# Leaving 48 instead of 32 tokens out of the dense expert pass of a PEER layer (one core)

## The chip, the cores and the metric

One core of a Trainium2 chip runs the whole program in one launch. The metric is the time of one execution in microseconds (us), the median over several executions. TensorE is called PE here, VectorE DVE, ScalarE ACT, GpSimd POOL and the sync engine's queue SP.

## What is computed

A residual block for 512 tokens of width 1024, in float32. After two kinds of attention and a LayerNorm comes a PEER layer: for every token, 8 heads choose 16 of 16384 experts each, so 128 experts a token, and sum their outputs.

```python
q = (xt @ w_q).reshape(T, PEER_HEADS, 2, half)
s1 = jnp.einsum('thd,hnd->thn', q[:, :, 0], keys1)
s2 = jnp.einsum('thd,hnd->thn', q[:, :, 1], keys2)
v1, i1 = lax.top_k(s1, 16); v2, i2 = lax.top_k(s2, 16)
cand = v1[..., :, None] + v2[..., None, :]         # 256 a head
sc, pos = lax.top_k(cand.reshape(T, 8, 256), 16)   # 16 experts a head, eidx
gate = jax.nn.softmax(sc, axis=-1)
a = jnp.einsum('nhkd,nd->nhk', u_tab[eidx], x)
w = jax.nn.gelu(a, approximate=False) * gate
y = jnp.einsum('nhk,nhkd->nd', w, v_tab[eidx])
x = layer_norm(ALPHA * x + y)
```

## The kernel before

The attention half ends at about 240 us and the change does not touch it. Then the 512 tokens are treated in two ways.

**Gathered tokens.** For the first 128 tokens (block 0, one token on each partition) the chosen rows of both tables are fetched. For each of the 128 ranks POOL issues one indirect DMA (line L822) that brings 128 rows of 4 KB, 0.524 MB, into one of 8 slots of `rows`. For `u_tab` DVE multiplies such a slot with x and sums it (`dot`, L1454), for `v_tab` it adds it with its weight to y (`add_row`, L1860). Of the 128 u ranks, 16 ("extra") are left for the second half of the program, where they have buffers of their own (`extra_row`, L864; `extra_dot_of`, L1848).

**Dense tokens.** For the other 384 tokens PE multiplies the whole table. The u pass goes over 128 tiles of 128 experts. Each tile is split into a high and a low float32r part (ACT `split_hi` L495, POOL `split_lo` L501, 4 slots ahead of PE), and `features` (L1964 to L1966) does 8 x 3 matmuls for it, whose moving side is the tokens. ACT takes the gelu (L1106) and stores it to DRAM. The gates of a chunk of 32 tokens are scattered into a dense array with one-hot matmuls: DVE builds the one-hots for groups of 8 tokens (`one_hots`, L1688 and L1692), PE multiplies them (`scatter`, L2237 and L2238), ACT stages the result and SP stores 2 MB a chunk. The v pass goes over 128 tiles too: DVE multiplies gelu and gate (L1802), the product is split (L1199, L1811), and PE adds 18 matmuls of 512 columns a tile (L2019 to L2021) into PSUM.

**Late tokens.** The last 32 of the 384 dense tokens are left out of the u pass, so a matmul there has 352 columns. In their 32 columns the gelu scratch holds ones. Their activations are computed from gathered rows: four groups of 32 partitions hold the same 32 tokens and a quarter of their ranks each, so 32 gathers and 32 dots do all of them. For this the numbers, the gates and at the end the products gelu x gate are moved between partitions (`move_numbers`, `move_gates`, `move_weights`, L625 to L645, four small copies from SBUF to SBUF each). The products are scattered in place of the gates, in the last groups of the last chunk, as three bf16 parts (`late_hots` L1717 and L1721, `late_scatter` L2251) and not two fp16 parts as in the other groups.

**The order.** Each engine runs its own list, written out by hand, and waits on semaphores. The u pass is: 44 tiles (`A_PRE`) beside which DVE finds the experts (`search_list`, `route_block`), six rounds of 12 tiles (`two_chunks`) with 8 scatter groups and 16 gathers each, and 12 last tiles. `turn_chosen` (L2212) transposes numbers and gates on PE at the first tile of round 0. `FIRST_GROUPS_AFTER = (2, 3, 4, 5)` puts the first four scatters of round 0 behind tiles 46 to 49; `GROUP_AFTER = (0, 1, 3, 4)` does it in every other half round. POOL gathers by tables: `FIRST_ROWS_AT` (32 rows at tiles 13 to 43), `LATE_ROWS` (round 0) and `MID_ROWS` (2, 1, 1, repeated). When the dots pass from one set of tokens to another, ACT copies the other x into PSUM (`home`, L1139) in front of a round. In the v pass an octet is 8 tiles with 8 v gathers, one load of gates (1.5 MB), two of gelus (0.75 MB) and 8 of v tiles (0.5 MB). `v_octet` (L866) and `octet` (L1870) take the extra ranks: two in octets 0 and 1, one in octets 2 to 13.

Of the kernel before, what the change touches and what calls it, by code (L numbers as in the profile page):

```python
# [103 lines left out]
LATE_ROWS = (0, 0, 0, 2, 3, 3, 2, 2, 2, 2, 2, 2)  # L104
# [4 lines left out]
SHARE_GAPS = 8, 9, 10  # L109
LIST_SLOTS = 4  # L110
# [14 lines left out]
def build(nc, x_t, x_rows, w1, w_ff, b_f, sinks, ln_par, w_pq, keys_t, u_t, u_rows, v_tab, consts, out):  # L125
    g_dram = nc.dram_tensor("g_scratch", (CHUNKS, P, ETILES, CHUNK), F32, kind="Internal").ap()
    a_dram = nc.dram_tensor("gelu_scratch", (ETILES // 4, P, 4, DENSE), F32, kind="Internal").ap()
    c_dram = nc.dram_tensor("decay_scratch", (4, HEADS, SEQ), F32R, kind="Internal").ap()

    ctx = ExitStack()  # L130
    with ctx:
# [106 lines left out]
        late_parts = row_weight[:, LATE_TOKENS:].bitcast(BF16).rearrange("p (m t two) -> p m t two", m=3, two=2)  # L238
# [136 lines left out]
        extra_gathered = [sem(f"extra_gathered{i}") for i in range(2)]  # L375
# [11 lines left out]
        late_numbers_ready = sem("late_numbers_ready")  # L387
        late_numbers_moved = sem("late_numbers_moved")
# [164 lines left out]
        EXTRA_ASKED_AT, EXTRA_DOT_AT = (2, 4), (5, 7)  # L553

        def extra_rows(j, par, at):

            if isinstance(j, int) and j == 0:
                return {k: (2 * par + i, i) for i, k in enumerate(at)}
            return {at[1]: (2 * j + (2 + par), par)}
# [18 lines left out]
        def _(sp):  # L578
# [1795 lines left out]
```

## Time and profile before

| what | value |
|---|---|
| time of the runs, median (range) | 1434.01 us (1432.85 to 1437.87) |
| time of the profiled execution | 1433.48 us |
| its span, first to last instruction | 1431.8 us |
| PE, PE weight loads, DVE | 1406.7, 1248.2, 1087.3 us busy |
| ACT, POOL | 606.7, 903.4 us busy |
| DMA | 415.41 MB in 138959 packets |

The profile names instructions by engine and line of the source, with what they write and read. A matmul row has the partitions and columns of what moves through PE; its duration reaches from the first column to a modelled end, and the next matmul starts well before it. So the pace of PE is read from the starts of successive rows. The brackets behind a row give how long the engine sat idle before it and what released it.

### The profile page before, as it was taken

The numbers are of one execution on the slowest core, as the hardware profiler recorded it, in microseconds if no ns is written. First come the engines' busy times: TensorE is split into PE (matmuls) and PEld (weight loads), VectorE is DVE, ScalarE is ACT, GpSimd is POOL, SyncE is SP. The second block draws the span as 40 slices with busy tenths as digits, with TensorE's granted clock in tenths as the row PEclk, the third lists the DMA queues.
The fourth block names the chain that finished last, engine by engine and source line by source line (L and its number), as shares of the span: only waits on it lengthen the run. The fifth ranks groups of instructions, "written<-read, shape, count | busy, mean of one in ns | idle before, by whom it ended". The sixth has DMA issues, their size and how long they took to land.

```text
span 1431.8 us, 24761 instructions
## 1 busy us (share of the span) xinstructions
PE 1406.7 (98%) x8045; PEld 1248.2 (87%) x8045; DVE 1087.3 (76%) x2324; ACT 606.7 (42%) x1019; POOL 903.4 (63%) x595
## 2 busy tenths in 40 slices
PE   9999999999999999999999999999999999999996
PEld 5888878888999999999999999878888888888885
DVE  5366666688999998858774885987777777777786
ACT  5666751324333354454544443333333333333332
POOL 3422331335599978979888786766666666666744
PEclk9999999999999999999999999999999999999998
DMA  6213120423689979999999899999999999999981
GB/s 243 75 50 113 59 90 1 147 84 102 197 316 342 323 259 395 417 389 418 418 417 399 341 381 407 383 388 387 371 374 374 372 366 360 367 368 366 372 315 59
DMA packets 138959, 415.41 MB, mean 290 GB/s; under 512 B 13904, under 2 KB 56656, under 8 KB 136720
## 3 DMA queue, kind: packets, MB, share of 16 engines
q1 hardware_dynamic: 80128, 240.69, 45.9%
q0 software_dynamic: 42064, 151.15, 26.8%
q10 hardware_dynamic: 16704, 22.81, 4.3%
q8 instruction: 29, 0.48, 0.1%
q14 instruction: 34, 0.28, 0.1%
HBM read 363.89 MB, written 50.14 MB: 289 GB/s over the span
## 4 chain that ended last, share of the span: by engine, by line
PE 76%; DVE 8%; DMA 5%; POOL 4%; issue 3%; ACT 2%; SPq 1%; DVEq 0%; ACTq 0%; POOLq 0%
PE banks L2019 12%; PE banks L2021 11%; PE banks L2020 11%; PE banks L1964 11%; PE banks L1965 11%; PE banks L1966 11%; DMA raw<-v_tab 3%; POOL lo L501 2%; PE banks L2081 2%; PE banks L2237 1%; PE banks L2238 1%; POOL rows L822 1%; PE banks L2174 1%; DMA rows<-u_rows,expert_at 1%; DVE rows L1454 1%
## 5 line engine op out<-in xcount | busy, mean ns | idle before, releaser
L501 POOL TENSOR_TENSOR lo<-raw,hi 128x1024 fp32r<-128x1024 f32 x224 | 540.2, 2413 | 416.5 <-ACT hi L495 396.5
L1964 PE MATMUL banks<-x1T_hi,hi 128*128 128x352 f32 (+3 forms) x1168 | 389.9, 334 | 1.3 <-ACT kept L1106 1.0
L1965 PE MATMUL banks<-x1T_lo,hi 128*128 128x352 f32 (+3 forms) x1168 | 384.6, 329 | 0.0
L1966 PE MATMUL banks<-x1T_hi,lo 128*128 128x352 f32 (+3 forms) x1168 | 383.6, 328 | 0.0
L495 ACT ACTIVATE hi<-raw 128x1024 fp32r<-128x1024 f32 x291 | 305.6, 1050 | 57.0 <-DMA raw<-u_t 37.4
L2019 PE MATMUL banks<-hi,wgt_hi 128*128 128x512 f32 x750 | 292.1, 389 | 2.0 <-DVE wgt_lo L1811 1.9
L2020 PE MATMUL banks<-lo,wgt_hi 128*128 128x512 f32 x750 | 291.8, 389 | 0.0
L2021 PE MATMUL banks<-hi,wgt_lo 128*128 128x512 f32 x750 | 291.8, 389 | 0.0
L1964 PEld LDWEIGHTS banks<-x1T_hi,hi 128*128 128x128 f32 x1168 | 219.8, 188 | 6.2 <-ACT kept L1106 1.3
L1966 PEld LDWEIGHTS banks<-x1T_hi,lo 128*128 128x128 f32 x1168 | 220.3, 189 | 4.4
L1965 PEld LDWEIGHTS banks<-x1T_lo,hi 128*128 128x128 f32 x1168 | 220.1, 188 | 3.9
L1454 DVE CUSTOM_DVE_ANT_0 rows<-rows,banks 128x1024 f32<-128x1024 f32 x144 | 172.5, 1215 | 61.0 <-DMA rows<-u_rows,expert_at 47.8
L1199 ACT ACTIVATE wgt_hi<-wgt 128x384 fp32r<-128x384 f32 x125 | 65.6, 525 | 313.1 <-PE banks L2021 284.4
L2019 PEld LDWEIGHTS banks<-hi,wgt_hi 128*128 128x128 f32 x750 | 140.8, 188 | 32.2 <-DVE wgt_lo L1811 2.7
L2021 PEld LDWEIGHTS banks<-hi,wgt_lo 128*128 128x128 f32 x750 | 140.8, 188 | 29.4
L2020 PEld LDWEIGHTS banks<-lo,wgt_hi 128*128 128x128 f32 x750 | 140.8, 188 | 29.2
L1860 DVE SCALAR_TENSOR_TENSOR banks<-rows,row_weight,banks 128x1024 f32<-128x1024 f32 x128 | 164.1, 1282 | 0.7
L822 POOL DMA_INDIRECT rows<-v_tab,expert_at x128 | 142.2, 1111 | 29.4 <-issue 21.1
L1811 DVE TENSOR_TENSOR wgt_lo<-wgt,wgt_hi 128x384 fp32r<-128x384 f32 x125 | 76.9, 616 | 108.6 <-ACT wgt_hi L1199 93.0
L822 POOL DMA_INDIRECT rows<-u_rows,expert_at x144 | 140.5, 975 | 28.8 <-issue 23.0
L1106 ACT ACTIVATE gelu<-banks 128x352 f32<-128x352 f32 x116 | 53.8, 464 | 241.4 <-PE banks L1966 229.1
L501 DVE TENSOR_TENSOR lo<-raw,hi 128x1024 fp32r<-128x1024 f32 x67 | 83.9, 1252 | 4.5 <-ACT hi L495 4.4
(245 smaller groups left out, 1846.7 us busy)
## 6 DMA issues: line engine op xcount, KB each, us to landing
raw<-u_t SPq DMA_DIRECT2D x128, 512.0 KB
raw<-v_tab SPq DMA_DIRECT2D x128, 512.0 KB
g_scratch<-stage SPq DMA_DIRECT2D x12, 2048.0 KB
gelu_scratch<-gelu ACTq DMA_DIRECT2D x116, 192.0 KB
ga<-gelu_scratch SPq DMA_DIRECT2D x29, 768.0 KB
gg<-g_scratch SPq DMA_DIRECT2D x14, 1536.0 KB
raw<-w SPq DMA_DIRECT2D x26, 512.0 KB
raw<-w_pq SPq DMA_DIRECT2D x16, 512.0 KB
```

What stands on the lines that cost most here:

```text
L495: act.activation(parts_of(c)[0][:, :], raw[:, c % RAW_SLOTS, :], ACT.Copy).then_inc(hi_ready, 1)
L501: eng.tensor_tensor(l[:, :], raw[:, c % RAW_SLOTS, :], h[:, :].bitcast(F32), ALU.subtract).then_inc(odd_lo_ready if by_vector(c) else lo_r ...
L822: pool.indirect_dma_start(rows[:, k % ROWS, :], None, table, at).then_inc(gathered[k % ROWS], 16)
L1454: dve.tensor_tensor_reduce(rows[:, k, :], rows[:, k, :], x1_home, 1.0, 0.0, ALU.mult, ALU.add, dots8[:, k:k + 1]).then_inc(row_used, 1)
L1811: dve.tensor_tensor(l[:, :], wgt[k % 2][:, :], h[:, :].bitcast(F32), ALU.subtract).then_inc(wgt_lo_ready, 1)
L1860: dve.scalar_tensor_tensor(y0, rows[:, k, :], row_weight[:, bass.ds(ROWS * r + k, 1)], y0, ALU.mult, ALU.add).then_inc(row_used, 1)
L1964: pe.matmul(o, h[:, s], hiT[:, k, tokens], start=(k == 0), stop=False)
L1965: pe.matmul(o, h[:, s], loT[:, k, tokens], start=False, stop=False)
L1966: ins = pe.matmul(o, l[:, s], hiT[:, k, tokens], start=False, stop=(k == KT - 1))
L2019: pe.matmul(o, h_at(b), h[:, s], start=start, stop=False)
L2020: pe.matmul(o, h_at(b), l[:, s], start=False, stop=False)
L2021: ins = pe.matmul(o, l_at(b), h[:, s], start=False, stop=stop)
```

## The change

It has five parts.

1. **48 late tokens.** `LATE_TOKENS` goes from 32 to 48 as `LATE_SETS = (32, 16)`. Matmuls of the u pass have 336 columns, gelu activations too, and 48 columns of ones stand in the scratch. The second set of 16 tokens lies eight times on the partitions, so 16 more u gathers and dots belong to late tokens, 48 in all.
2. **16 extra ranks more for the v pass.** `EXTRA` goes from 16 to 32, so the u pass still has 144 gathers and dots. In the v pass an octet takes 2 extra ranks in octets 0 and 1, 3 in octets 2 to 5 and 2 in octets 6 to 13. A third buffer (`extra2`) lies over the gelu slots. The ranks are turned into weights in two batches of 16.
3. **Transfers through DRAM.** Numbers, gates and weights are stored to DRAM with one DMA for each set and loaded in the other layout with another. The x of the second set is stored eight times in front of the u pass and loaded in round 0 into `sel`.
4. **Order.** `turn_chosen` goes from tile 44 to tile 45, the first dots of round 0 go behind one more group of one-hots (`FIRST_DOTS`), and `LATE_ROWS` starts one tile later. There are homes for x before rounds 0, 2 and now 3, and the weights are stored in round 4 and not behind round 2.
5. **Two more late groups.** 6 instead of 4 of the last 8 scatter groups are late ones, and `late_part_free` lets a late group use one-hot buffers of the round before.

```diff
-LATE_TOKENS = 32
-SPREAD = P // LATE_TOKENS
+LATE_SETS = (32, 16)
+LATE_TOKENS = sum(LATE_SETS)
 LATE_AT = P - LATE_TOKENS
-LATE_RANKS = RANKS // SPREAD
+LATE_RANKS = sum(RANKS // (P // n) for n in LATE_SETS)
 FEATURED = DENSE - LATE_TOKENS
-EXTRA = 16
+EXTRA = 32
+EXTRA_BATCHES = (16, 16)
...
-LATE_ROWS = (0, 0, 0, 2, 3, 3, 2, 2, 2, 2, 2, 2)
+LATE_ROWS = (0, 0, 0, 0, 2, 3, 3, 3, 3, 2, 2, 2)
+FIRST_DOTS = (0, 2, 2, 2, 2, 3, 2, 3)
+CHOSEN_AT = 1
+FIRST_BATCH_AT = 8
...
             n = 3 * (group - WHOLE_GROUPS) + m
-            used_by = n // 2 if n < len(late_slots) else WHOLE_GROUPS + (n - len(late_slots)) // 3
+            if n < len(late_slots):
+                used_by = n // 2 - (HOT_SLOTS if n // 2 >= WHOLE_GROUPS else 0)
+            else:
+                used_by = WHOLE_GROUPS + (n - len(late_slots)) // 3
             return 2 * (used_by + 1)
...
-        EXTRA_ASKED_AT, EXTRA_DOT_AT = (2, 4), (5, 7)
+        ASKED_AT = {2: (2, 4), 3: (0, 2, 4)}
+        DOT_AT = {2: (4, 6), 3: (2, 4, 6)}
...
-            def move_numbers():
+            def store_numbers():
 
                 sp.wait_ge(late_numbers_ready, 1)
-                for g in range(SPREAD):
-                    sp.dma_start(late_numbers[late_group(g), :],
-                                 block_numbers[LATE_AT:, late_group(g)]).then_inc(late_numbers_moved, 16)
+                for i, n, tokens, columns in late_sets():
+                    sp.dma_start(turn_dram[0][i].rearrange("g t c -> t g c"),
+                                 block_numbers[tokens, :].rearrange("t (g c) -> t g c", c=n)
+                                 ).then_inc(late_numbers_stored, 16)
+
+            def load_numbers():
+
+                sp.wait_ge(late_numbers_stored, 16 * LATE_MOVES)
+                for i, n, tokens, columns in late_sets():
+                    sp.dma_start(late_numbers[:, columns], turn_dram[0][i].rearrange("g t c -> (g t) c")
+                                 ).then_inc(late_numbers_moved, 16)
...
-                        if first and tile == 0:
+                        if first and tile == CHOSEN_AT:
                             take_turned()
...
-            v_octet(0, 0)
-            v_octet(0, 1)
-            with pool.Fori(1, OCTETS // 2 - 1) as i:
-                v_octet(i, 0)
-                v_octet(i, 1)
+            v_octet(0, 0, 2)
+            v_octet(0, 1, 2)
+
+            for slot in range(GELU_SLOTS):
+                pool.wait_ge(gelu_stored[slot], 16 * (A_PRE + A_MID) // GELU_SLOTS)
+            with pool.Fori(1, 3) as i:
+                v_octet(i, 0, 3)
+                v_octet(i, 1, 3)
+            with pool.Fori(3, OCTETS // 2 - 1) as i:
+                v_octet(i, 0, 2)
+                v_octet(i, 1, 2)
...
-                    if first and tile == 0:
+                    if first and tile == CHOSEN_AT:
                         turn_chosen(at)
```

**First place: the start of round 0 on DVE.** `is_i` are the one-hots of the numbers, `gate_hi` and `gate_lo` those times the gates; the first row copies the gates to PSUM. Before:

```order
L1669 COPY banks<-gate_lo 128x384 [waits gate_step]
L1688 TENSOR_TENSOR is_i_0<-banks,selT 128x1024 [waits gate_step]
L1692 TENSOR_TENSOR gate_hi<-is_i_0,banks 128x1024 [waits is_i1_ready]
L1692 TENSOR_TENSOR gate_lo<-is_i_0,banks 128x1024
L1688 TENSOR_TENSOR is_i_0<-banks,selT 128x1024 [waits onehot_ready]
L1688 TENSOR_TENSOR is_i_1<-banks,selT 128x1024
L1454 ISA rows,small<-rows,banks 128x1024 [waits dots8_free,gathered0,homes_ready]
```

And with the change, from the same copy on:

```order
L1766 COPY banks<-gate_lo 128x384 [waits gate_step]
L1785 TENSOR_TENSOR is_i_0<-banks,selT 128x1024 [waits gate_step]
L1789 TENSOR_TENSOR gate_hi<-is_i_0,banks 128x1024 [waits is_i1_ready]
L1789 TENSOR_TENSOR gate_lo<-is_i_0,banks 128x1024
L1785 TENSOR_TENSOR is_i_0<-banks,selT 128x1024 [waits onehot_ready,homes_ready]
L1785 TENSOR_TENSOR is_i_2<-banks,selT 128x1024
L1551 ISA rows,small<-rows,banks 128x1024 [waits dots8_free,gathered0]
```

The third group's one-hots now stand in front of the first dot. Nothing in front of the first group moved (some repeated rows between are not shown).

**Second place: the last round on DVE,** from the second group of one-hots on. Before, it is followed by dots and by two more groups of this kind:

```order
L1747 CAST row_weight<-small 128x64 [waits late_step]
L1688 TENSOR_TENSOR is_i_0<-banks,selT 128x1024 [waits onehot_ready,scattered,late_step]
L1688 TENSOR_TENSOR is_i_1<-banks,selT 128x1024
L1692 TENSOR_TENSOR gate_hi<-is_i_0,banks 128x1024 [waits is_i1_ready]
L1692 TENSOR_TENSOR gate_lo<-is_i_0,banks 128x1024
```

With the change the group behind its dots is already a late one:

```order
L1814 TENSOR_TENSOR is_i_0<-banks,selT 128x1024 [waits onehot_ready,scattered]
L1814 TENSOR_TENSOR is_i_2<-banks,selT 128x1024
L1818 TENSOR_TENSOR gate_hi<-is_i_0,sel 128x1024 [waits scattered,is_i1_ready]
L1818 TENSOR_TENSOR gate_lo<-is_i_0,sel 128x1024 [waits scattered]
L1818 TENSOR_TENSOR gate_hi<-is_i_0,sel 128x1024 [waits scattered]
```

Groups 2 and 3 have three products instead of two, each with a wait for PE, and the parts they read lie in `sel`.

## Rows read from the trace of the kernel before

**Rows 1.** Windows: length, busy PE, PEld, DVE, ACT, POOL, clock, DMA share, GB/s.
```profile
600.00:760.00 160.00, 160.00 (x1240) 156.88 (x1239) 121.29 (x206) 76.87 (x123) 136.45 (x92) 1.00 1.01 411
893.00:970.00 77.00, 75.03 (x330) 61.23 (x329) 69.41 (x76) 26.72 (x36) 53.25 (x40) 1.00 1.02 387
1099.60:1132.20 32.60, 32.60 (x146) 26.99 (x145) 24.61 (x31) 11.82 (x16) 20.73 (x16) 1.00 0.98 372
1130.00:1140.00 10.00, 10.00 (x46) 8.29 (x45) 7.42 (x10) 3.59 (x5) 7.62 (x5) 1.00 1.03 421
```

**Rows 2.** Timeline of PE: start, duration; first and last of 36, 21 and 45 matmuls.
```profile
599.74 0.32 PE L1964 MATMUL banks<-x1T_hi,hi 128*128 128x352 f32 x1
605.34 0.32 PE L1966 MATMUL banks<-x1T_hi,lo 128*128 128x352 f32 x1
...
329.95 0.39 PE L1964 MATMUL banks<-x1T_hi,hi 128*128 128x512 f32 x1
334.48 0.39 PE L1966 MATMUL banks<-x1T_hi,lo 128*128 128x512 f32 x1
...
252.21 0.27 PE L1964 MATMUL banks<-x1T_hi,hi 128*128 128x128 f32 x1
257.12 0.27 PE L1966 MATMUL banks<-x1T_hi,lo 128*128 128x128 f32 x1
```

**Rows 3.** Timeline of DVE from the last routing steps to the first one-hots.
```profile
516.63 0.68 DVE L1639 TENSOR_TENSOR sel<-sel,gsum 128x512 f32<-128x512 f32 x1
517.23 2.48 DVE L1612 SCALAR_TENSOR_TENSOR dots_gelu<-sel 128x128 f32<-128x128 f32 x1
524.65 2.30 DVE L1664 CAST gate_hi<-selT 128x768 f16<-128x768 f32 x1
530.85 0.68 DVE L1692 TENSOR_TENSOR gate_lo<-is_i,banks 128x1024 f16<-128x1024 f16 x1
```

**Rows 4.** What DVE waited for from 350 to 530 us: total, times, longest.
```profile
DVE best L1487 <- ACT scores L1074: 0.6, 1, 0.6
DVE work L1584 <- DVE cand L1579: 0.5, 1, 0.5
```

**Rows 5.** Timeline of PE: the first scatter.
```profile
532.39 0.23 PE L2237 MATMUL banks<-gate_hi,is_i 128*128 128x128 f16 x1
```

**Rows 6.** Timeline of POOL: splits, gathers and its wait for the numbers.
```profile
455.37 2.41 POOL L501 TENSOR_TENSOR lo<-raw,hi 128x1024 fp32r<-128x1024 f32 x1
457.94 0.96 POOL L822 DMA_INDIRECT rows<-u_rows,expert_at  x1 [0.16 <-issue]
458.92 4.77 POOL L501 TENSOR_TENSOR lo<-raw,hi 128x1024 fp32r<-128x1024 f32 x2
523.86 0.19 POOL L815 COPY expert_at<-small 128x8 uint32<-128x8 uint32 x1 [4.29 <-DMA small<-row_weight]
```

**Rows 7.** Timeline of the last round: ACT, DVE, then PE.
```profile
791.70 0.18 ACT L1192 ACTIVATE small<-banks 128x32 f32<-128x32 f32 x1
793.07 1.29 DVE L1688 TENSOR_TENSOR is_i<-banks,selT 128x1024 f16<-128x1024 f16 x2
794.87 0.68 DVE L1692 TENSOR_TENSOR gate_lo<-is_i,banks 128x1024 f16<-128x1024 f16 x1
809.81 3.29 DVE L1721 TENSOR_TENSOR gate_hi<-is_i,row_weight 128x1024 bf16<-128x1024 bf16 x1
833.35 3.29 DVE L1721 TENSOR_TENSOR gate_lo<-is_i,row_weight 128x1024 bf16<-128x1024 bf16 x1
840.84 0.23 PE L2251 MATMUL banks<-gate_lo,is_i 128*128 128x128 bf16 x1
842.13 0.22 PE L2251 MATMUL banks<-gate_lo,is_i 128*128 128x128 bf16 x1
```

**Rows 8.** Waits of ACT: the first from 866 to 900 us, the second from 900 to 1000.
```profile
ACT hi L495 <- DMA raw<-u_t: 11.9, 4, 6.7
...
ACT hi L495 <- DMA raw<-v_tab: 9.5, 4, 4.4
```

More of the change, by code:

```diff
@@ L551, in shared_norm, with extra_number_of, early_extras, late_sets @@
             return SHARED.index(n)
-        EXTRA_ASKED_AT, EXTRA_DOT_AT = (2, 4), (5, 7)
[L555 to L559, printed above, removed]
+        ASKED_AT = {2: (2, 4), 3: (0, 2, 4)}
+        DOT_AT = {2: (4, 6), 3: (2, 4, 6)}
+        def extra_number_of(i, each, q):
+            return (2 * i + (EXTRA_BATCHES[0] - 12 + q) if each == 2 else 3 * i + (q - 2)) if not early_extras(i) else 2 * i + q
+        def early_extras(i):
+            return isinstance(i, int) and i < 2
+        def late_sets():
+            first, column = P, 0
+            for i, n in enumerate(LATE_SETS):
+                first -= n
+                yield i, n, slice(first, first + n), slice(column, column + n)
+                column += n
         def lagging(step, lag, j, first):
@@ L647, in two_chunks @@
+            def two_chunks(o, first=False, weights=False):
                 for t in range(MID_TILES):
@@ L1161, in late_dots_done, with two_chunks @@
                 act.activation(late_gelu, late_dots, ACT.Gelu).then_inc(late_gelu_ready, 1)
-            def two_chunks(o, first=False, second=False, last=False):
+            def two_chunks(o, first=False, second=False, third=False, last=False):
                 for half in range(2):
@@ L1176, in two_chunks @@
                         if second and tile == 0:
+                            second_home()
+                        if third and tile == 0:
                             late_dots_done()
@@ L1750, in _, with two_chunks @@
             one_hots(0, 0, True)
-            def two_chunks(o, first=False, second=False, last=False):
+            def two_chunks(o, homes=None, first=False, last=False):
                 for tile in range(8):
@@ L1758, in two_chunks @@
                         one_hots(tile + 1, o, first and tile + 1 < HOT_SLOTS)
-                    if first and tile == 0:
-                        dve.wait_ge(homes_ready, 3)
-                    if second and tile == 0:
-                        dve.wait_ge(homes_ready, 4)
-                    for n in (2 * tile, 2 * tile + 1):
+                    if homes is not None and tile == 0:
+                        dve.wait_ge(homes_ready, homes)
+                    done = sum(FIRST_DOTS[:tile]) if first else 2 * tile
+                    for n in range(done, done + (FIRST_DOTS[tile] if first else 2)):
                         dot(n % ROWS, 2 * o + (R_PRE + n // ROWS))
@@ L2257, in two_chunks @@
                     at = tile % 4, 3 * o + (A_PRE // 4 + tile // 4)
-                    if first and tile == 0:
+                    if first and tile == CHOSEN_AT:
                         turn_chosen(at)
```

192 lines of the change are left out of this document (129 added, 63 removed).

## The prediction

> **What bounds the kernel now.** I read the busy times first, then windows and pace, then who waits for whom. PE is busy nearly all the time, and between 600 and 760 us all of it [rows 1], so the time is PE's list plus its few stalls. A busy PE tells nothing of its pace; that is read from starts [rows 2]. In the u pass 36 matmuls of 352 columns start within 5.60 us, one each 160.0 ns. With 512 columns it is 4.53 us for 20 steps, 226.5 ns. The slope is 66.5 ns for 160 columns, 0.416 ns a column. The next limits stand close behind. In front of round 0 it is DVE: from 350 to 530 us it waited 0.6 us at most for anything [rows 4], so the end of routing and the first one-hots come when DVE has done its list, whatever PE does. POOL is second: a split and a gather take 2.41 and 0.96 us with small gaps, 3.55 us a tile (455.37 to 458.92) [rows 6], against 24 x 0.160 = 3.84 us of PE. Third are the DMA engines, with shares of 0.98 to 1.03 from round 1 to the end [rows 1].
>
> **Part 1, the columns (-20.4 us).** A matmul loses 16 columns, 16 x 0.416 = 6.65 ns, a tile 0.16 us, so it takes 3.68 us; 128 tiles x 24 = 3072 matmuls give 20.4 us. This holds if the pace follows the columns down to 336. What could forbid it is the weight load, which every matmul keeps whatever its columns. PE's weight loads are busy 156.88 of 160 us in the u pass [rows 1]. But matmuls of 128 columns, with loads of the same size, start each 111.6 ns [rows 2], far under the 153 ns wanted here, so the loads overlap. The Trainium skill, page Perfetto Trace Analysis, section Identifying the Most-Contended Engine, judges TensorE by the busy share of its weight loads. By it PE is at 98% of a limit that the change doesn't touch, and part 1 would be nothing; that is rival C.
>
> **Front of round 0 (+5.6 us).** PE's first scatter stands behind tile 46 before and after and needs the first one-hots. DVE ended them at 530.85 + 0.68 = 531.5 us [rows 3], PE started at 532.4 [rows 5]. With the change PE would come 47 x 0.16 = 7.5 us earlier, but in DVE's list nothing in front of these one-hots has moved, only behind them. So PE waits until 531.5 at the latest: 0.9 us of the 7.5 stay, 6.6 are lost. Two rows of DVE are much longer than their size asks for: 2.48 us for 128 elements, 2.30 us for a cast [rows 3], both while POOL splits. POOL's next split now waits longer for the late numbers, and one of the two may come free, about 1 us. I take a loss of 5.6, bounds 4 and 7.5. Moving the transposes to tile 45 costs nothing: that wait was under 1 us, and PE now waits at the scatter. POOL's stalls at tiles 13 to 21 (a tile with two gathers costs it about 4.8 us against 3.68) are covered by the same wait.
>
> **Late numbers and gathers (+1.0 us).** POOL waited 4.29 us for the numbers, until 523.86 [rows 6]. Now two stores, a wait and two loads stand in that place, and SP has them in front of its next tile loads. No row shows a load behind a store here; the nearest is that POOL wait, the whole of a copy with its four issues, so I put the numbers 0 to 4.3 us later, at about 526. In front of tile 55 POOL then has 2, 3, 3, 3, 3, 2, 2 gathers, 18 x 1.25 us, and 8 splits x 2.41: it ends the split of tile 55 at about 568, and PE wants it at about 568. Queued behind it is only the next split. I take 1 us, bounds 0 and 3. The gates, the second x, its home before round 3 and the weights have a round of slack each: nothing, since DVE is busy 121.29 of 160 us [rows 1].
>
> **Two more late groups (+0.9 us on PE).** 24 matmuls instead of 16 a group: 1.29 us for 23 steps, 56 ns each [rows 7], 16 x 56 = 0.9 us.
>
> **The same on DVE (+3.5 us).** In the last round DVE may start only when ACT has taken the weights (791.70). A normal group takes 793.07 to 795.5, 2.4 us; the late ones take 5.9, 6.4, 4.3 and 5.8, mean 5.6, because some products last 3.29 instead of 0.68 us [rows 7]. DVE ended the last at 833.35 + 3.29 = 836.6, PE wanted it at 840.84, 4.2 us later [rows 7]. Two groups turned late add 2 x 3.2 = 6.4 us to DVE, and the first one's third product waits for scatter 1, 0.5 us. PE comes 11 x 0.16 = 1.8 us earlier and is 0.9 longer. Stall: 6.9 - 4.2 + 1.8 - 0.9 = 3.6, say 3.5. Bounds: 0, if the products fall beside POOL's work more luckily (0.68 each), and 6.
>
> **From the last round to octet 1 (+2.5 us).** ACT waited for tiles 11.9 and 9.5 us here [rows 8], PE stood 1.97 of 77 us between 893 and 970, at a DMA share of 1.02 [rows 1]. The bytes stay the same, so the 12 last u tiles can't come in 1.9 us less, and DVE starts its last 16 dots later. I take 2.5, bounds 0 and 5.
>
> **The extra ranks (+4 us).** 16 more gathers of 0.524 MB; at the 421 GB/s of a full window [rows 1] each takes 1.25 us of all engines. An octet takes 32.6 us and moves 372 GB/s at a share of 0.98 [rows 1]; full windows read 1.02 to 1.03, so 4 to 5%, 1.3 to 1.7 us, are free. One more rank (octets 6 to 13) just fits. Two more (octets 2 to 5) are 2.5 us, over by 0.8 to 1.2, times 4 octets, with no slack carried from before since PE stood before 970. I take 4, bounds 0 and 20 (16 x 1.25, nothing free). DVE and POOL have room: 24.61 and 20.73 of 32.6 us [rows 1], plus at most 2 x 2.5 us each.
>
> **Sum.** 1433.5 of the profiled execution - 20.4 + 5.6 + 1.0 + 0.9 + 3.5 + 2.5 + 4.0 = 1431.1 - 0.5 for stalls counted twice (a PE that waits in one place lets the DMA engines catch up for the next) = 1430.6 us. That execution is 0.5 us under the median of the runs, which I leave alone.
>
> **Rivals.** *A: the queues absorb it.* The stalls of the last round, of the way to octet 1 and of the v pass stay near nothing, since tiles are split 4 ahead and loads have several us of slack; then 1433.5 - 20.4 + 5.6 + 1.0 + 0.9 = 1420.6, about 1422. For it: PE is busy through the whole octet shown, at 372 GB/s where another window moves 421 [rows 1]. Against: the shares near 1. The same section of the Trainium skill's page calls the occupancy of the 16 DMA engines misleading and goes by bandwidth; by it 12% are free and every extra rank fits, which is this rival. Chance 0.20.
>
> *B: the v pass becomes DMA-bound, slower.* The place is octets 2 to 13, the price 1.25 us for each of 16 ranks. It decides from the point at which the share of 0.98 means that nothing is free: then all octets stretch, and instead of 4 us it is 16 to 20. 1430.6 + 12 = 1442.6. For it: the window at 1.02 already had PE standing. Against: another reads 1.03 with 421 GB/s [rows 1]. Chance 0.20.
>
> *C: PE is bound by weight loads.* Part 1 is 0, and so are the losses that come from an earlier PE: 1433.5 + 0.9 + 2 + 4 = 1440.4. Against it the 111.6 ns. Chance 0.03.
>
> *D: gathers fall behind in rounds 0 and 1,* since POOL has 0.1 us of slack a tile instead of 0.3: up to 5 us more, 1435.6. Chance 0.07.
>
> **Chances.** What a measurement of this kernel can tell from no change is about 0.3%, 4.3 us: faster is under 1429.7, slower over 1438.3. My forecast has 0.50, and since its terms scatter by some us and its value lies near that line, 0.17 of it is faster and 0.33 the same. A gives 0.20 faster, B 0.18 slower and 0.02 the same, C 0.03 slower, D 0.05 the same and 0.02 slower. Sum: faster 0.37, same 0.40, slower 0.23. The range reaches to A and to B, 1421 to 1443; the forecast's own is 1426 to 1436.
>
> **What would show it.** Starts of 336-column matmuls each 153 ns. PE idle by 4 to 7 us just before its first scatter, with DVE's one-hots as releaser. POOL's wait for the numbers ending near 526. In the last round PE waits for late one-hots of groups 5 to 7. From 970 to about 1090 us PE shows small stalls and DMA shares over 1.0, with 400 GB/s. I am wrong if the pace stays at 160 ns, if the first scatter comes well before 530 us, or if the v pass takes 1.5% more or not a bit more than before.

## The result and the profile after

| | median us | runs | ratio to before, 95% interval |
|---|---|---|---|
| before | 1434.4 | 1432.85 to 1437.87 | |
| the change | 1461.8 | 1458.45 to 1468.88 | 1.0199, 1.0166 to 1.0233 |

The change makes the kernel 2.0% slower, where 1430.6 us was forecast. The profiled execution of the changed kernel spans 1467.2 us (time 1468.88) against 1431.8, 35.4 us more. It is the longest of the four runs; by the medians the loss is 27.4. From here on all stretches are of profiled executions, and the table places the 35.4 us: u tiles by the start of their gelu on ACT, octets by the start of their first cast of the weights on ACT.

| point | before | after | lag | lost on the way | predicted loss |
|---|---|---|---|---|---|
| u tile 0 | 353.3 | 352.8 | -0.5 | | |
| u tile 49 | 547.0 | 544.6 | -2.4 | 5.9 | 5.6 |
| u tile 56 | 578.8 | 581.1 | +2.3 | 5.8 | 1.0 |
| u tile 102 | 785.6 | 781.5 | -4.1 | 1.0 | 0 |
| u tile 105 | 799.3 | 801.1 | +1.8 | 6.4 | 0 |
| u tile 116 | 850.1 | 851.1 | +1.0 | 1.0 | 4.4 |
| u tile 127 | 893.7 | 898.1 | +4.4 | 5.2 | 2.5 |
| end | 1431.8 | 1467.2 | +35.4 | 31.0 | 4 |

"Lost" is the change of the lag plus the 0.16 us that each tile should gain. The gain itself is there. In the timeline of PE in the changed kernel (start, duration) these are the first and last of 17 matmuls, 2.46 / 16 = 153.8 ns each against 160.0 in [rows 2]. Undisturbed gelus of the last 12 tiles follow each other in 3.68 us instead of 3.84, so 127 tiles bring 20.3 us.

```profile
564.74 0.31 PE L2075 MATMUL banks<-x1T_lo,hi 128*128 128x336 f32 x1
...
567.20 0.32 PE L2076 MATMUL banks<-x1T_hi,lo 128*128 128x336 f32 x1
```

All of it and 35 us more is lost. Of the 31.0 us behind the last u tile, 3.0 are lost before octet 2, 26.1 in octets 2 to 14, and 2.0 in the end of the program, which no run isolates. The octets:

| octet | 0 | 1 | 2 | 3 to 5 | 6 to 12 | 13 | 14 |
|---|---|---|---|---|---|---|---|
| before | 32.9 | 33.8 | 33.8 | 32.64 | 32.64 | 32.7 | 32.6 |
| after | 36.4 | 32.6 | 35.0 | 34.0 to 34.2 | 35.0 to 35.2 | 34.5 | 34.1 |
| extra ranks after (before) | 2 | 2 | 3 (1) | 3 (1) | 2 (1) | 2 (1) | 0 |

Octets 3 to 5 with three extra ranks lose less than octets 6 to 12 with two. The bytes of the ranks alone can't do that. The window of one octet of the changed kernel, to be read against the third line of [rows 1] (busy PE, PEld, DVE, ACT, POOL, then clock, DMA share, GB/s):

```profile
1171.50:1206.70 35.20, 33.29 (x146) 26.91 (x146) 28.89 (x36) 11.86 (x17) 23.56 (x17) 1.00 0.94 359
```

PE stands 1.9 of 35.2 us, and the DMA engines move less than before, 359 GB/s at 0.94 instead of 372 at 0.98. Neither DVE (28.9) nor POOL (23.6) is full. So this is a chain of waits. The waits of that octet (total, times, longest), and of PE from 1000 to 1415 us:

```profile
POOL lo L524 <- ACT hi L518: 9.1, 3, 4.4
ACT wgt_hi L1286 <- DVE wgt L1899: 8.2, 2, 4.7
DVE extra L1945 <- DMA extra<-u_rows,small: 2.3, 1, 2.3
PE banks L2129 <- DVE wgt_lo L1908: 1.9, 2, 1.5
...
PE banks L2129 <- DVE wgt_lo L1908: 18.9, 19, 1.5
```

The timeline of the octet, first POOL's, then DVE's:

```profile
1178.53 1.80 POOL L936 DMA_INDIRECT extra<-u_rows,small  x1 [0.30 <-issue]
1186.63 1.86 POOL L936 DMA_INDIRECT extra<-u_rows,small  x1 [0.30 <-issue]
1189.41 2.40 POOL L524 TENSOR_TENSOR lo<-raw,hi 128x1024 fp32r<-128x1024 f32 x1 [0.92 <-ACT hi L518]
1199.39 2.40 POOL L524 TENSOR_TENSOR lo<-raw,hi 128x1024 fp32r<-128x1024 f32 x1 [4.43 <-ACT hi L518]
...
1190.03 2.86 DVE L1945 CUSTOM_DVE_ANT_0 extra<-extra,x 128x1024 f32<-128x1024 f32 x1 [2.35 <-DMA extra<-u_rows,small]
1192.82 0.55 DVE L1908 TENSOR_TENSOR wgt_lo<-wgt,wgt_hi 128x384 fp32r<-128x384 f32 x1
1198.27 1.21 DVE L1945 CUSTOM_DVE_ANT_0 extra<-extra,x 128x1024 f32<-128x1024 f32 x1
1199.42 2.78 DVE L1908 TENSOR_TENSOR wgt_lo<-wgt,wgt_hi 128x384 fp32r<-128x384 f32 x1
```

POOL asks for the first extra row at 1178.53. Its dot stands two tiles later in DVE's order, behind tile 4, and DVE reaches it 9.2 us after the ask; the row lands 11.5 us after it, at 1190.03. DVE has stood 2.35 us with the weights of tile 4 queued behind. It then runs beside POOL's splits: the dot takes 2.86 us instead of 1.21, a `wgt_lo` 2.78 instead of 0.55. POOL's split had begun 0.03 us ahead of that one and lasted 2.40; DVE's instruction ended 0.4 us behind it. The Trainium skill, page SBUF — State Buffer, section SBUF: two separate sides, says that a shared port pair is an exclusive lock: a DVE operation with two SBUF inputs or a GpSimd operation that reads SBUF, whichever starts first, has it for the whole instruction, and the other fully blocks. These rows agree: `wgt_lo` reads `wgt` and `wgt_hi`, and it ended 0.4 us behind the split. PE waits 1.5 and 0.4 us in this octet, both times for a `wgt_lo`. The end of this chain, shares of the span, on the changed kernel's page:

```profile
PE 26%; DVE 23%; DMA 17%; issue 17%; POOL 12%; ACT 3%; DVEq 0%; POOLq 0%; SPq 0%; ACTq 0%
```

In the u pass the losses sit at tiles 55 and 103 and at the end. Windows of the changed kernel there (columns as above), and what PE waited for from 778 to 800 us:

```profile
576.00:584.00 8.00, 5.79 (x47) 5.32 (x45) 8.00 (x13) 3.66 (x7) 7.57 (x6) 0.99 1.03 417
584.00:588.00 4.00, 3.51 (x25) 3.51 (x26) 3.98 (x9) 1.26 (x3) 3.52 (x4) 0.59 1.04 418
784.00:788.00 4.00, 2.08 (x14) 1.80 (x12) 0.00 (x0) 0.12 (x1) 0.99 (x2) 1.00 1.04 419
788.00:792.00 4.00, 2.44 (x9) 2.47 (x10) 0.21 (x1) 3.40 (x6) 2.84 (x2) 0.59 1.02 415
792.00:796.00 4.00, 4.00 (x18) 4.00 (x17) 3.85 (x9) 0.00 (x0) 0.48 (x1) 0.56 1.04 416
796.00:800.00 4.00, 4.00 (x37) 3.88 (x36) 4.00 (x7) 2.37 (x4) 2.24 (x2) 1.00 0.28 103
...
PE banks L2388 <- ACT stage L1230: 3.5, 1, 3.5
```

PE stands 2.2 us from 576 to 584 and 3.5 from 784 to 792. Behind each stall the granted clock is 0.56 to 0.59 for 4 and 8 us, near the lower of its two levels (1.2 of 2.4 GHz), and that costs again: 18 matmuls start from 792 to 796, 37 from 796 to 800. PE waited for ACT, and ACT for tiles:

```profile
574.79 1.06 ACT L518 ACTIVATE hi<-raw 128x1024 fp32r<-128x1024 f32 x1 [6.79 <-issue]
787.88 1.06 ACT L518 ACTIVATE hi<-raw 128x1024 fp32r<-128x1024 f32 x1 [5.97 <-DMA raw<-u_t]
```

(The first wait has the label issue, so the trace doesn't show what ended it. ACT's next ones, until 589 us, are for tiles, and the DMA engines are full, with a share of 1.03 from 576 on.) One round of the u pass, tiles 90 to 102, in DMA numbers, before and after:

```profile
DMA packets 6201, 21.80 MB, mean 404 GB/s; under 512 B 689, under 2 KB 2224, under 8 KB 5944
DMA packets 6710, 21.75 MB, mean 418 GB/s; under 512 B 1267, under 2 KB 2722, under 8 KB 6455
```

Before, a round moved 21.8 MB in 53.9 us. Now it moves as much in 52.0 at 418 GB/s; no window of 52 us that was read went over 419. And 52.0 us is also PE's own list of a round (8 tiles of 4.66 us, 4 of 3.68). Such windows between 604 and 797 us read 399 to 419 GB/s (before 395 to 419, with 1.9 us more for each round), so little slack is left from round 0 on, and none where it is 418.

### The profile page after: what moved, and what is told of

Read it like the earlier page. It is cut to its first block, busy times and chain, and to the rows that moved or that the text cites. A ratio compares the mean times of both kernels' runs of the same rounds, so it can differ in the third digit from the quotient of the medians.

```text
span 1467.2 us, 24512 instructions
## 1 busy us (share of the span) xinstructions
PE 1403.4 (96%) x8061; PEld 1234.3 (84%) x8061; DVE 1143.4 (78%) x2375; ACT 608.4 (41%) x1021; POOL 922.1 (63%) x627
## 4 chain that ended last, share of the span: by engine, by line
PE 26%; DVE 23%; DMA 17%; issue 17%; POOL 12%; ACT 3%; DVEq 0%; POOLq 0%; SPq 0%; ACTq 0%
DMA extra<-u_rows,small 8%; POOL lo L524 6%; POOL rows L893 6%; DMA raw<-u_t 5%; PE banks L2074 4%; PE banks L2076 4%; PE banks L2075 4%; PE banks L2129 3%; PE banks L2131 3%; PE banks L2130 3%; DMA rows<-u_rows,expert_at 2%; DVE banks L1957 2%; DVE rows L1551 2%; PE banks L2191 2%; DVE wgt L1899 2%
## 5 line engine op out<-in xcount | busy, mean ns | idle before, releaser
L524 POOL TENSOR_TENSOR lo<-raw,hi 128x1024 fp32r<-128x1024 f32 x224 | 546.5, 2442 | 415.8 <-ACT hi L518 390.4
L2074 PE MATMUL banks<-x1T_hi,hi 128*128 128x336 f32 (+3 forms) x1168 | 385.1, 330 | 8.8 <-POOL lo L524 4.1
L2076 PE MATMUL banks<-x1T_hi,lo 128*128 128x336 f32 (+3 forms) x1168 | 378.8, 324 | 0.0
L2075 PE MATMUL banks<-x1T_lo,hi 128*128 128x336 f32 (+3 forms) x1168 | 378.0, 324 | 0.0
L2129 PE MATMUL banks<-hi,wgt_hi 128*128 128x512 f32 x750 | 295.2, 394 | 24.5 <-DVE wgt_lo L1908 24.5
L893 POOL DMA_INDIRECT rows<-v_tab,expert_at x128 | 137.4, 1073 | 32.3 <-issue 21.3
L1908 DVE TENSOR_TENSOR wgt_lo<-wgt,wgt_hi 128x384 fp32r<-128x384 f32 x125 | 103.5, 829 | 63.5 <-ACT wgt_hi L1286 37.0
L1184 ACT ACTIVATE gelu<-banks 128x336 f32<-128x336 f32 x116 | 52.2, 450 | 184.8 <-PE banks L2076 169.7
```

Of the source, the lines that this page charges most:

```text
L524: eng.tensor_tensor(l[:, :], raw[:, c % RAW_SLOTS, :], h[:, :].bitcast(F32), ALU.subtract).then_inc(odd_lo_ready if by_vector(c) else lo_r ...
L893: pool.indirect_dma_start(rows[:, k % ROWS, :], None, table, at).then_inc(gathered[k % ROWS], 16)
L1908: dve.tensor_tensor(l[:, :], wgt[k % 2][:, :], h[:, :].bitcast(F32), ALU.subtract).then_inc(wgt_lo_ready, 1)
L2074: pe.matmul(o, h[:, s], hiT[:, k, tokens], start=(k == 0), stop=False)
L2075: pe.matmul(o, h[:, s], loT[:, k, tokens], start=False, stop=False)
L2076: ins = pe.matmul(o, l[:, s], hiT[:, k, tokens], start=False, stop=(k == KT - 1))
```

## The experiments

Every kernel ran beside the kernel before on the same chip. Theory P: the place of the dots in DVE's order makes the v pass slow. Rivals: B, bytes; Q, no room on DVE and POOL. For the u pass: D, bytes; W, R, S and N, order of SP's queue.

**v_odd: the dots one tile later.**

```diff
-        DOT_AT = {2: (4, 6), 3: (2, 4, 6)}
+        DOT_AT = {2: (5, 7), 3: (3, 5, 7)}
```

> The changed kernel (1461.8 us) with the dots of the extra rows one tile later, behind tiles 5 and 7 (3, 5 and 7 in the octets with three) instead of 4 and 6 (2, 4, 6). Bytes, gathers and DVE's work are the same. Theory P (place): a gather of an extra row lands about 10 to 11.5 us after POOL asks for it, two tiles of the v pass are 8.2 us, so DVE stands at its dot with two weights queued behind it, and the even tile holds a split as well. With three tiles (12.2 us) between and no split in the tile, an octet with two extra ranks falls from 35.1 us to 32.7 to 33.3, with three from 34.1 to 32.7 to 33.5; the time to about 1438, 1432 to 1445. Theory B (the v pass is bound by the DMA engines, rival B of the prediction): the same bytes need the same time, octets stay at 34 to 35 us, 1458 to 1464. Theory Q (DVE and POOL together have no room for two dots an octet, wherever they stand): the octets of two ranks stay over 34.3 us, time above 1452.

1443.6 us (1441.6 to 1443.8), ratio to before 1.0061, 1.0042 to 1.0079: 18 us of the 27 come back. Octets 7 to 13 take 32.64 to 32.70, exactly as before, with one extra gather more. One of them, in v_odd, windows and the first gather with its dot 12.2 us behind:

```profile
1195.40:1228.00 32.60, 32.60 (x145) 27.02 (x144) 26.48 (x35) 11.80 (x16) 22.19 (x18) 1.00 1.01 392
...
1202.15 0.94 POOL L936 DMA_INDIRECT extra<-u_rows,small  x1 [0.30 <-issue]
1214.38 2.35 DVE L1945 CUSTOM_DVE_ANT_0 extra<-extra,x 128x1024 f32<-128x1024 f32 x1
```

392 GB/s at a share of 1.01 and PE never stands. B falls, and so does Q, for two ranks. Octets 2 to 6 take 33.3 to 35.7, and POOL, not DVE, waits there (from 990 us on):

```profile
POOL small L931 <- DVE small L1945: 15.5, 3, 5.2
```

With three buffers POOL still asks only when the dot two back is done. Then its split comes late, beside DVE's products.

**v_ask_early: the gathers one of POOL's steps (two tiles) earlier, dots left on even tiles.**

```diff
-        ASKED_AT = {2: (2, 4), 3: (0, 2, 4)}
+        ASKED_AT = {2: (0, 2), 3: (0, 2, 4)}
```

> The changed kernel with the gathers of the extra rows asked for at POOL's steps 0 and 2 instead of 2 and 4 in the octets with two (0, 1 and 6 to 13); the dots stay behind tiles 4 and 6, where DVE splits a v tile too. The octets with three are as they were and serve as a control, 34.1 us. Theory P in its form 'the landing is late': the wait of DVE for the extra row goes, octets 6 to 13 fall from 35.1 to 33.0 us or under, 8 x 2 = 16 us or more less, 1440 to 1447. In its form 'an even tile has no room for a dot' (split 1.2, product and two casts 2.3, dot 1.2 to 2.9 us against 4.08): the octets fall by less than half of that, to 34 us or more, 1452 to 1458. Theory B: no change, 1458 to 1464.

1446.7 us (1445.5 to 1449.3), 1.0083, 1.0066 to 1.0101. Octets 6 to 13: 32.64 to 32.70. The control octets 3 to 5 stay at 33.9 to 34.5. The dot now stands 17.3 us behind its ask. So an even tile has room for the dot; it is the landing that is late.

```profile
1200.17 1.88 POOL L936 DMA_INDIRECT extra<-u_rows,small  x1 [0.30 <-issue]
1217.48 1.22 DVE L1945 CUSTOM_DVE_ANT_0 extra<-extra,x 128x1024 f32<-128x1024 f32 x1
```

**b_even_dot: the kernel before with its dots on the even tiles.**

```diff
-        EXTRA_ASKED_AT, EXTRA_DOT_AT = (2, 4), (5, 7)
+        EXTRA_ASKED_AT, EXTRA_DOT_AT = (2, 4), (4, 6)
```

> The kernel before (1434.4 us) with one edit: the dots of the extra rows behind tiles 4 and 6 instead of 5 and 7; 16 extra ranks, one an octet. Theory P: the place alone costs, since the row asked at POOL's step 4 has 8.2 us instead of 12.2 and the tile holds a split: each of 14 octets gets longer by 1 to 2.5 us, time up by 15 to 35 us, 1449 to 1469. Theory B: the place costs nothing, 1432 to 1437. Theory Q in the middle: one dot an octet fits anywhere since DVE has 8 us an octet, up by less than 5 us.

1433.45 us (1431.6 to 1436.2), 0.9994, 0.9984 to 1.0004: nothing. My form of P was wrong here. With one gather an octet the row is there 9.3 us after the ask, and DVE doesn't wait:

```profile
1170.76 0.94 POOL L864 DMA_INDIRECT extra<-u_rows,small  x1 [0.30 <-issue]
1180.04 1.22 DVE L1848 CUSTOM_DVE_ANT_0 extra<-extra,x 128x1024 f32<-128x1024 f32 x1
```

Its octets 0 and 1 hold two extra ranks each, and there DVE does wait once in each, for rows that land 10.4 and 10.9 us after the ask. So the place costs only together with a gather that lands later than the 8 to 9 us it gives; and what sets the landing is open at this point.

**w_load_later: SP never stands at the stored weights.**

```diff
-                    if weights and t == 2:
+                    if weights and t == 4:
                         load_weights()
```

> The changed kernel with one edit in the u pass: SP loads the late weights back from DRAM behind the tile load of step 4 of round 4 instead of step 2. Theory W: in the changed kernel SP stood about 7 us (754 to 761) at the wait for the stores, with the tile loads queued behind it, ACT then waited 6.0 us for a tile at 787.9, PE stood at the late product and ran 8 us at the lower clock, and the 12 last u tiles, which the DMA engines bound, came later by as much. Without the standing the round 5 start loses 1 us instead of 6.4, and the u pass ends 4 to 8 us earlier: 1453 to 1458. Rival R (the wait for late products and one-hots at the start of round 5 bounds it whatever the tile loads do): the tile loads come on time and the time falls by at most 1.5 us, 1460 to 1463. Rival: the weights come later than PE wants them (781 us), time up by 1 to 4 us.

1463.6 us (1462.1 to 1465.9), 1.0209, 1.0191 to 1.0228. SP went on without standing (its four tile loads follow at the pace of the slots), and ACT waited all the same:

```profile
751.76 12.23 SPq L506 DMA_DIRECT2D raw<-u_t  x4
764.03 0.91 SPq L706 DMA_DIRECT2D dots_gelu<-late_weight_scratch  x2
...
788.82 1.06 ACT L518 ACTIVATE hi<-raw 128x1024 fp32r<-128x1024 f32 x1 [5.44 <-DMA raw<-u_t]
```

W falls. R isn't borne out either, since the tile loads didn't come on time. The 7 us of SP (754 to 761) looked like the cause and were not.

**u_336: fewer bytes.** The scratch loses the 48 columns of ones; they are set once in the two buffers of the v pass.

```diff
-    a_dram = nc.dram_tensor("gelu_scratch", (ETILES // 4, P, 4, DENSE), ...
+    a_dram = nc.dram_tensor("gelu_scratch", (ETILES // 4, P, 4, FEATURED), ...
...
-                    act.dma_start(a_dram[it, :, k, :], gelu[k][:, :])
+                    act.dma_start(a_dram[it, :, k, :], gelu[k][:, 0:FEATURED])
...
-                    sp.dma_start(ga[slot][:, :, :], a_dram[g])
+                    sp.dma_start(ga[slot][:, :, 0:FEATURED], a_dram[g])
...
+            for slot in range(2):
+                dve.memset(ga[slot][:, :, FEATURED:DENSE], 1.0)
```

> The changed kernel with the gelu scratch cut to the 336 columns that a tile has; the ones stand in the two buffers that the v pass reads it into. 24.6 KB less a tile are stored, 2.9 MB in the u pass, and as many less read in the v pass. Theory D (the u pass from round 0 on is bound by the DMA engines at about 418 GB/s: a round moves 21.8 MB, 52.1 us, and PE's list of a round is 52.0): 0.7 us less of transfers a round, the stalls near tiles 55, 103 and 121 to 124 get smaller by 3 to 7 us together; the last u tile's gelu starts at 888 to 893 us instead of 893 to 898 (four runs of this u pass: 898.1, 896.2, 895.2, 893.3), time 1455 to 1460. Theory N (the stalls come from SP's order and the late products, not from bytes): 894 to 898, time 1459 to 1464. A cost of the smaller pieces (1344 bytes instead of 1536 and 6144) would show as a higher share at lower GB/s.

1440.5 us (1437.8 to 1447.3), 1.0054, 1.0028 to 1.0079, far better than I expected: 21 us. The u pass did as D said (last gelu at 891.5; tiles 102 to 105 in 13.6 us, where PE's list is 13.0). In the 52 us up to tile 102 the DMA engines still move 21.7 MB at 418 GB/s, so there they stay full and are only less behind. The rest came in the v pass, which I had not foreseen: octets 2 to 4 with three ranks take 32.64, octets 5 to 12 take 33.5 to 34.0 instead of 34.1 to 35.2, and octet 7 32.65. In two neighbouring octets of this kernel the asks of the first rows and their dots are:

```profile
1129.51 2.02 POOL L936 DMA_INDIRECT extra<-u_rows,small  x1 [0.30 <-issue]
1138.88 1.23 DVE L1947 CUSTOM_DVE_ANT_0 extra<-extra,x 128x1024 f32<-128x1024 f32 x1
...
1162.14 0.94 POOL L936 DMA_INDIRECT extra<-u_rows,small  x1 [0.30 <-issue]
1172.36 1.23 DVE L1947 CUSTOM_DVE_ANT_0 extra<-extra,x 128x1024 f32<-128x1024 f32 x1 [0.79 <-DMA extra<-u_rows,small]
```

In the first the dot starts 9.4 us after the ask without a wait, and the octet takes 32.65 us. In the second the row lands after 10.2 us, 0.79 late, and it takes 33.5. In octets 6 to 13 the first row landed 9.7 to 10.2 us after its ask where DVE waited for it, and 11.0 to 11.5 in the changed kernel. So the landing is quicker with fewer bytes, and the changed kernel sat over the edge. The Trainium skill, page Perfetto Trace Analysis, section DMA Instruction — SWDGE (GPSIMD), says that the row of such an instruction ends when its descriptors are written and not when the data has moved; the rows agree, 0.94 to 2.0 us for the row and 9 to 11.5 to the dot that can start.

**u_second: the second x a round later** (its load from step 8 of round 0 to step 3 of round 1).

> The changed kernel with the load of the second x (0.5 MB) moved from step 8 of round 0 to step 3 of round 1, where nothing needs it before round 2. Theory S: it helps tile 55, which came at 576.7 instead of 568: the stretch from tile 54 to 56 takes 10 to 12 us instead of 12.4 to 13.6. Theory D (backlog of all transfers of round 0, the gathers three a tile at tiles 53 to 56 first of all, which stand before it in time): the stretch stays at 12 to 14 us, since the load stands behind tile 56's.

1463.7 us (one run): tiles 54 to 56 in 13.2 us, as in the changed kernel (13.6). S falls.

**v_late3: two extra ranks in octets 0 to 9, three in 10 to 13; POOL looks three dots back where three buffers are in use.**

```diff
-            with pool.Fori(1, 3) as i:
-                v_octet(i, 0, 3)
-                v_octet(i, 1, 3)
-            with pool.Fori(3, OCTETS // 2 - 1) as i:
+            with pool.Fori(1, 5) as i:
                 v_octet(i, 0, 2)
                 v_octet(i, 1, 2)
+            for i in range(5, OCTETS // 2 - 1):
+                v_octet(i, 0, 3)
+                v_octet(i, 1, 3)
...
-                    pool.wait_ge(extra_used, n - 1)
+                    pool.wait_ge(extra_used, n - (back - 1))
```

> The changed kernel with the dots on the odd tiles as in the run v_odd (1443.6 us), and the four octets with three extra ranks moved from octets 2 to 5 to octets 10 to 13; there POOL asks for a row when the dot three back is done (its buffer is free), not two back. Same bytes, gathers and dots. In v_odd octets 2 to 5 took 33.3 to 35.7 us against 32.64, 8.9 us in all, POOL waiting up to 5.2 us for a dot and its splits then falling beside DVE's products. Theory O (the order of POOL and DVE: three dots do not fit while POOL waits for the dot two back): with two an octet and the third one later all octets take 32.6 to 33.0, v pass as long as before, time 1434 to 1438. Theory B3 (three extra ranks an octet are over what the DMA engines give, wherever they stand): octets 2 to 5 fall to 32.64, octets 10 to 13 rise to 33.5 to 35, time 1437 to 1444.

1436.9 us (1435.1 to 1442.6), 1.0022, 1.0009 to 1.0034. Octets 2 to 9 and 11 to 13 take 32.4 to 32.7, three ranks included; B3 falls. O fits, but the place of the octets and the look back were changed together, so it isn't shown what each is worth. Octet 10, where POOL still looks two dots back, takes 34.9.

**best1: v_late3 and u_336.**

> v_late3 and u_336 together: the changed kernel with the dots placed anew and the gelu scratch of 336 columns. If both theories (order of the dots; bytes in the u pass) hold, the savings add: 1427 to 1434, level with the kernel before or up to 0.5% faster. If u_336 gives nothing, 1434 to 1438.

1433.4 us (1432.2 to 1435.7), 0.9993, 0.9984 to 1.0003. Octet 10 again 34.85, because its second row takes the buffer whose dot stands behind tile 7 of octet 9. POOL in best1:

```profile
1227.81 0.18 POOL L931 COPY small<-expert 128x1 uint32<-128x1 uint32 x1 [3.35 <-DVE small L1947]
1228.33 2.41 POOL L524 TENSOR_TENSOR lo<-raw,hi 128x1024 fp32r<-128x1024 f32 x1
```

**best2: the buffers in the order 2, 0, 1 from octet 10 on**, so that the free one is taken first (`slot_of(each, q)` gives `(2, 0, 1)[q]` for three ranks). The edit also lets POOL look three dots back in octet 10, as in 11 to 13.

> best1 (1433.4 us) with the three buffers of the extra rows taken in the order 2, 0, 1 in octets 10 to 13, so that the first of octet 10 takes the buffer that is free. In best1 POOL waited 3.3 us in octet 10 for the dot behind tile 7 of octet 9, its splits then fell beside DVE's products, and the octet took 34.85 us; octet 14 took 34.9 from a similar start. Theory O: octet 10 falls to 32.7 to 33.2, and octet 14 may too: 1429 to 1432. Rival: three gathers an octet cost the 2 us by their bytes, octet 10 or 11 stays near 34.8, 1433.

1432.0 us (1428.6 to 1438.0), 0.9993, 0.9980 to 1.0007. Octet 10: 32.64, and all from 2 to 14 (13: 32.70). The trace shows it; the ratio is that of best1, so the time alone doesn't.

**best3: the split of tile 48 ahead of the wait for the late numbers.**

```diff
-                gather(u_rows, ranks, 0, (S_U + k, 0))
+                gather(u_rows, ranks, 0, (S_U + k, 0), split_first=t == LATE_ROWS.index(2))
```

> best2 with one edit more, in round 0: POOL splits tile 48 ahead of its wait for the late numbers (7.4 us until 526.5 in the changed kernel) instead of behind it. From 520 to 536 us the DMA engines had shares of 0.40 and 0.74, since the split frees a place for the next tile load and nothing was asked for meanwhile; 50 us later PE stood near tile 55 for tiles that the DMA engines brought late. Theory D: the idle transfers are made up earlier, the stretch from tile 54 to 56 falls from 12.9 us by 2 to 4, time 2 to 4 us under best2. Theory N: the backlog at tile 55 comes from the gathers that POOL asks for behind the numbers, which come 2.4 us earlier at most: no change within 1 us.

1429.3 us (1428.1 to 1430.7), 0.9967, 0.9955 to 0.9980. POOL's wait in the changed kernel and in best3, and the window from 520 to 528 in both:

```profile
526.53 0.19 POOL L886 COPY expert_at<-small 128x8 uint32<-128x8 uint32 x1 [7.36 <-DMA small<-late_number_scratch]
520.00:528.00 8.00, 8.00 (x56) 7.98 (x55) 7.86 (x15) 4.68 (x7) 1.38 (x2) 1.00 0.40 127
```

```profile
520.55 2.39 POOL L524 TENSOR_TENSOR lo<-raw,hi 128x1024 fp32r<-128x1024 f32 x1 [1.28 <-ACT hi L518]
527.45 0.19 POOL L889 COPY expert_at<-small 128x8 uint32<-128x8 uint32 x1 [4.50 <-DMA small<-late_number_scratch]
520.00:528.00 8.00, 8.00 (x56) 7.98 (x57) 7.83 (x16) 4.78 (x7) 2.58 (x2) 1.00 0.58 170
```

The DMA engines move 170 GB/s instead of 127 in the hole, and tile 56 comes at 578.5 instead of 580.8 (best2). The time fell as D said. The stretch from tile 54 to 56 fell from 13.3 to 11.9 us, by 1.4, less than D's 2 to 4 and more than N's 1; the other 0.9 had come before tile 54. This kernel is 0.3% faster than before and 2.2% faster than the change.

**b_352: the kernel before with its scratch cut to 352 columns.**

> The kernel before with the gelu scratch cut to its 352 columns in the same way (16.4 KB less a tile each way). Control: there PE, not the DMA engines, bounds the rounds (53.9 us a round against 52.1 that the bytes need), so the time falls by 0 to 1.5 us, from the 12 last u tiles: 1433 to 1434.5. If it fell by 4 us or more, the saving in the changed kernel would be nothing of the 48 tokens' own.

1434.2 us (1431.5 to 1439.7), 1.0001, 0.9989 to 1.0014. Where PE bounds the rounds the bytes are worth nothing.

**order_only: best3 with the scratch of 384 columns.**

> best3 (1429.3 us) with the gelu scratch of the changed kernel again (384 columns): all edits of order (dots on odd tiles, octets with three late, buffers 2, 0, 1, split ahead of the numbers) and none of bytes. The runs so far give v_late3 1436.9, which lost 2.2 us in octet 10 that the buffer order takes away, and 2.7 us between best2 and best3 for the split. If order and bytes add: 1436.9 - 2.2 - 2.7 = 1432.0, 1431 to 1434, so that the bytes are worth 2.5 to 4 us. If the bytes matter only where order is bad, it is 1429 to 1430.5; if the u pass falls back to stalls near tile 103 as in the changed kernel, 1434 to 1437.

1434.5 us (1430.0 to 1438.6), 0.9993, 0.9979 to 1.0006, 5.2 us over best3 by the medians and 3.7 by the ratios. Tiles 102 to 105 took 16.8 us. Over all kernels of the change with 384 columns (seven) this stretch took 15.0 to 19.7 us, over the four with 336 columns 13.3 to 13.7. The two profiled executions are 9.6 us apart, and only 2.5 of that arise between the first u tile and the first weights; 2.1 lie ahead of the first u tile, 2.2 in octets 0 and 1 and 2.8 in octet 14.

## Why the prediction was wrong

- **Part 1, the columns:** right in pace, 153.8 ns for 153.3. Rival C (weight loads) is out: they are busy 51.07 of 52.0 us in the round from tile 90 on, 98% as before, and the pace fell all the same.
- **Front of round 0:** 5.9 for 5.6 us, though not as described. PE waited only 1.7 us at the first scatter, until 530.0 where I had 531.5. Between tiles 13 and 25 it had lost 3.8 us, 2.7 of them in waits for POOL's splits, which I had said the wait at the scatter would cover. They took its place. That the number came out is in part luck.

```profile
530.04 0.23 PE L2347 MATMUL banks<-gate_hi,is_i 128*128 128x128 f16 x1 [1.68 <-DVE gate_lo L1789]
```

- **Late numbers:** at 526.5 for 526. The right wait, but its price was mis-sized. I looked at what POOL does next and not at what its split holds up, the tile loads. The DMA engines idled, and 5.8 us came out near tile 55 instead of 1.0. best3 gives back 2.3 of them; what the rest is due to (the gathers three a tile, the bytes of the round) isn't separated.
- **The byte limit of the rounds:** I wrote "the bytes stay the same, so the 12 last u tiles can't come in 1.9 us less" and used it for those 12 tiles alone. With 411 GB/s in [rows 1] and 21.8 MB a round it bore on every round: an undisturbed round still kept PE's pace, but little could be made up. Tiles 103 to 105 lost 6.4 us, the most of all executions: kernels with the same 384 columns lose 2.0 to 6.7 us there against the list of 13.0, those with 336 lose 0.3 to 0.7. That is what the bytes do; what else moves it between 2.0 and 6.7 is open. The gates, second x and weights got "a round of slack each: nothing": that held for their order (w_load_later, u_second).
- **Last round:** 3.5 us for the late groups on DVE did not come. PE waited for none of their one-hots, being late itself. In v_late3 it came 5 us earlier, and tiles 105 to 116 took 50.2 us where its list is 49.9 (50.8 of before - 1.8 + 0.9). So the 0.9 on PE did come. (The four late groups of before read 6.0, 6.5, 4.4 and 5.9 us, 0.1 more each than I wrote; that changes nothing.)
- **From the last round to octet 1:** 2.5 us forecast, 5.2 lost by the last u tile and 3.0 more before octet 2. In u_336 the last u tile came 6.6 us earlier, so the bytes bear on it. Octet 0 took 33.2 to 37.3 us in kernels of the change that differ little there. What decides it stays open.
- **The extra ranks: this step failed.** I priced an extra rank by the transfer time alone, 1.25 us, and closed DVE and POOL with "have room: 24.61 and 20.73 of 32.6 us, plus at most 2 x 2.5". A sum of busy times says nothing of a dot that stands in order two tiles behind its gather. The diff showed the step: from (2, 4) asked and (5, 7) used to (4, 6) used, one tile less, 4.08 us. In its place the runs show a wait of DVE for the row, which landed 11.0 to 11.5 us after the ask in octets 6 to 13 where DVE was there after 9.2, and POOL's and DVE's instructions then falling together. Octets 2 to 13 lost 24.6 us instead of 4 (31.0 from the last u tile to the end). v_odd, v_ask_early and u_336 take 18, 15 and 21 us of the 27 away (u_336 some of it in the u pass), by a later dot, an earlier ask, and a quicker landing. By b_even_dot the place alone costs nothing with one rank an octet: it takes the place and the later landing together.
- **Rival B** named a slower v pass, at 1442.6, but by bytes; v_odd and v_late3 show octets of two and three extra ranks at 32.64 us. **Rival A** was right that they fit: by its rule (bandwidth, not occupancy, the Trainium skill's page Perfetto Trace Analysis, section Identifying the Most-Contended Engine) there was room, and octets ran at 392 GB/s with a share of 1.01. It was wrong for the u pass, where 418 GB/s was the top over a round. Rival D came nearest for round 0, with the wrong engine.

## What to carry over

A gather costs its transfer and a distance: count the time from the ask to the in-order instruction that needs it, in tiles, and compare it with the longest landing under load, not with an idle one. Where an engine's own time shrinks, divide the bytes of a whole period by the best rate any window shows; if that equals the new period, a later stall can't be made up. And of a wait that gets longer, ask what the waiting engine would have set free.

## What was not expected of the hardware

- The landing of a gather of 0.5 MB took under 9.4 us in b_even_dot and in octet 7 of u_336, 10.2 in its octet 8 and 11.5 in the changed kernel, at DMA rates that differ little. These are the windows from ask to dot, in this order (columns as above):

```profile
1170.76:1180.04 9.28, 9.28 (x42) 7.68 (x42) 6.75 (x9) 2.96 (x4) 5.39 (x4) 1.00 1.00 396
1129.51:1138.88 9.37, 9.37 (x43) 7.74 (x42) 6.78 (x9) 2.96 (x4) 8.13 (x7) 1.00 1.05 409
1162.14:1172.36 10.22, 10.22 (x46) 8.46 (x46) 6.90 (x10) 3.65 (x6) 6.90 (x7) 1.00 1.04 399
1178.53:1190.03 11.50, 11.50 (x52) 9.52 (x52) 6.57 (x8) 4.43 (x6) 9.34 (x8) 1.00 1.03 408
```

  It is not isolated how much of this is the queue ahead of the gather and how much POOL's later descriptors (rows of 0.94 to 2.02 us, and the longest row isn't that of the slowest landing).
- A late DVE can stay late. Octet 14 has no extra rank and took 32.64 us in some kernels and 34.1 to 35.4 in others (34.9 in best1, 32.64 in best2, from the same code there). In the slow ones that I read (best1, order_only, u_336 and the changed kernel) POOL's splits fell beside DVE's `wgt_lo` one to three times, 2.7 us for 0.55, and in best2 never. That this keeps DVE late is argued from the rows, and what starts it wasn't isolated.
- Stalls of PE of 2 to 4 us were followed by 4 to 8 us at a granted clock of 0.56 to 0.59.
